# One opening stage for a two-block network's kernel: set-up, first modulation, scales and norm merged, loads in another order, the step-size products moved behind the first weight slot

## The chip, the cores and the metric

The kernel runs on one core of one Trainium2 chip. A core has TensorE (PE in the profile, matmuls; its weight loads are listed apart as PEld), VectorE (DVE), ScalarE (ACT), GpSimd (POOL) and SyncE (SP, which here only issues DMA transfers). The metric is the device time of one execution in microseconds, lower is better: the median of 3 runs is 2491.7 us (2485.37 to 2492.45).

## The reference, cut to what matters

The network is two blocks on x of 256 tokens by 1024 features. The change is at the very start of the first one: the modulation of layer 0, its RMS norm, and the first projection of the hybrid mixer.

```python
cs = jax.nn.silu(c)                                    # c: 1024 values
mod = cs @ ada_w[0] + ada_b[0]                         # 6 x 1024 values
sh1, sc1, g1, sh2, sc2, g2 = split(mod, 6)
h = rms_norm(x, norm_mix_g[0]) * (1 + sc1) + sh1       # rms_norm = x * rsqrt(mean(x*x) + 1e-6) * g
x = x + g1 * hybrid_mixer(h, hy_w_in, ...)             # starts with h @ hy_w_in: z, xBC, dt, q, k, v
...                                                    # ffn, conformer layer, ffn, second block
```

`dt` is the mixer's step size, 32 columns of the projection. `rel_table` gives the attention's bias by distance; the kernel looks it up with one small product against a one-hot matrix.

## The kernel before, in words

All data is fp32, with features on the 128 partitions: x and h are tiles [128, 8, 256]. Weights stream from memory as slots of 128 x 4096 values (2 MB) through a ring of four buffers. `slot_landed[n]` counts their arrival, `slot_used` counts how many were consumed, and SP issues the load of slot n+4 when slot n has been used (`load_ahead`, L97). SP issues everything for the ring, one after the other, on one DMA queue; POOL issues other loads on its own queue.

The program is a row of stages. Each is a `Block` with one instruction list for each engine, and no engine starts a stage before all engines have ended the one before (the branch with which an engine enters a stage waits on a barrier of all five). Within a stage only semaphores order the engines. The stages at the start are:

1. `stage_setup` (L131): SP issues the loads of the vector c (`y<-in_cvec`, copied to all partitions), of ring slots 0 to 3, of the parameters `par`, of the constants `con` and of x, in this order. ACT waits for c, par and con together (`landed`, 48) and applies silu to c.
2. `stage_mod` (L159): DVE computes 16 columns of shift and scale from ring slots 0 to 3, four tiles of 128 x 1024 for each slot (`mod_tile`, L154: multiply and sum in one instruction, written over the weights, followed by a short read of the sum). SP loads the next four slots, the first four of the in-projection, as the ring comes free.
3. `stage_scales` (L255): one DVE instruction, gain = (1 + scale) * g.
4. `stage_norm` (L188, body L193 to L252): ACT squares x in two halves; PE first runs `keep_warm` (two 128x512 products whose result nobody reads), then sums the squares by eight products with a matrix of ones, then seven more `keep_warm` products; DVE scales the sum, ACT takes the root, DVE the reciprocal and x * rstd, and the eight tiles of h are made by DVE and ACT, four each.
5. `stage_hyin` (L280): SP loads `wdt`, the weights of the step sizes, and three small tables. PE computes the step-size products (L339, 16 products 128x32), the look-up (L343), and then ten slots of the in-projection (L271, 32 products of 128x256 for each slot) into two alternating pairs of PSUM banks. DVE copies the step sizes and the masked bias, then for each slot does two modulation tiles of the later columns (weights by POOL's queue), two convolution steps and the copy of one bank; ACT copies the other bank. The third slot's products wait for the first slot's two copies, and so on. After its last ring load SP stores the masked bias (`bias_table`), which the stage waits for at its end.

An fp32 product appears in the trace as two PE records: 32 products of a slot are 64 records.

Of the kernel before, what the change touches and what calls it, by code (L numbers as in the profile page):

```python
# [91 lines left out]
def wait_slot(k, eng, n, turn=0):  # L92

    eng.wait_ge(k.slot_landed[n % RING], turn * 16 + 16 * (n // RING + 1))
# [27 lines left out]
def row(k, name, i=0, n=1):  # L122
    c = PAR[name] + i
    return k.par[:, c:c + n]


def const(k, name):
    return k.con[:, CON[name]:CON[name] + P]


def stage_setup(nc, k, a, cvec):  # L131

    with ExitStack() as ctx:
        landed = ctx.enter_context(nc.semaphore("setup_landed"))
        silu_done = ctx.enter_context(nc.semaphore("setup_silu"))
        block = ctx.enter_context(nc.Block())

        @block.sync
        def _(sp):
            sp.dma_start(cvec, a["cvec"][:, 0:D].to_broadcast([P, D])).then_inc(landed, 16)  # L140
            for n in range(RING):
                sp.dma_start(k.ring[:, n, :], k.stream[n]).then_inc(k.slot_landed[n], 16)
            sp.dma_start(k.par[:], a["par"]).then_inc(landed, 16)
            sp.dma_start(k.con[:], a["con"]).then_inc(landed, 16)
            sp.dma_start(k.x[:], a["xt"]).then_inc(k.x_landed, 16)
            sp.wait_ge(landed, 48)

        @block.scalar
        def _(act):
            act.wait_ge(landed, 48)  # L150
            nc.scalar.activation(cvec, cvec, ACT.Silu).then_inc(silu_done, 1)


def mod_tile(nc, products, w, vec, out, bias):  # L154

    return nc.vector.tensor_tensor_reduce(products, w, vec, 1.0, bias, ALU.mult, ALU.add, out)  # L156


def stage_mod(nc, k, first, vec, out, bias):  # L159


    with ExitStack() as ctx:
        block = ctx.enter_context(nc.Block())

        @block.sync
        def _(sp):
            load_ahead(k, sp, first, RING)
            sp.wait_ge(k.x_landed, 16)

        @block.vector  # L170
        def _(dve):
            for j in range(RING):
                wait_slot(k, dve, first + j)
                w = k.ring[:, (first + j) % RING, :]
                for q in range(4):
                    c = 4 * j + q
                    wt = w[:, q * D:(q + 1) * D]
                    ins = mod_tile(nc, wt, wt, vec, out[:, c:c + 1], bias[:, c:c + 1])
                ins.then_inc(k.slot_used, 1)


def keep_warm(k, pe, bank, n):

    for _ in range(n):
        pe.matmul(k.psum[bank][:], const(k, "ident"), k.con[:, 0:512], start=True, stop=True)  # L185


def stage_norm(nc, k, src, nt, width, scale, bias, dst, name):  # L188
# [91 lines left out]
def stage_hyin(nc, k, h, y, a, dtok, vec, table):  # L280
# [7 lines left out]
    with ExitStack() as ctx:  # L288
# [44 lines left out]
        @block.tensor  # L333
        def _(pe):
            rhs = [h[:, kt, :] for kt in range(KT)]
            pe.wait_ge(wdt_landed, 16)
            for c in range(2):
                for kt in range(KT):
                    mm = pe.matmul(k.psum[7][:, c * HEADS:(c + 1) * HEADS], h[:, kt, c * P:(c + 1) * P],  # L339
                                   wdt[:, kt, :], start=(kt == 0), stop=(kt == KT - 1))  # L340
            mm.then_inc(dt_done, 1)
            pe.wait_ge(bias_in, 48)
            pe.matmul(k.psum[6][0:48, 0:384], rel[:], onehot[:], start=True, stop=True).then_inc(looked_up, 1)  # L343
            for n in range(NFIRST):
                if n >= 2:
                    pe.wait_ge(stored_dve, n - 1)
                    pe.wait_ge(stored_act, n - 1)
                b = 2 * (n % 2)
                outs = [k.psum[b + i // 2][:, (i % 2) * T:(i % 2 + 1) * T] for i in range(4)]
                slot_products(k, pe, first + n, 0, rhs, outs).then_inc(k.slot_used, 1)  # L350

        @block.vector
        def _(dve):
            dve.wait_ge(dt_done, 1)
            nc.vector.tensor_copy(dtok[:], k.psum[7][:, 0:2 * HEADS])
            dve.wait_ge(looked_up, 1)
            nc.vector.scalar_tensor_tensor(flat[:], k.psum[6][0:48, 0:384], 8.0, neg[:], ALU.mult, ALU.add).then_inc(
                bias_masked, 1)

            def half_slot(n):  # L360
                dve.wait_ge(mod_landed, 16 * (n + 1))
# [28 lines left out]
            for n in range(NFIRST):  # L390
                for half in range(*HALVES[n]):
                    half_slot(half)
                for p in turns(n):
                    convolve(p)
                dve.wait_ge(k.slot_used, first + n + 1)
                nc.vector.tensor_copy(y[:, place(n):place(n) + 2, :],
                                      k.psum[2 * (n % 2)].rearrange("p (i t) -> p i t", i=2)).then_inc(stored_dve, 1)

        @block.scalar
        def _(act):  # L400
# [2225 lines left out]
def first_block(nc, k, a):  # L2626
    with ExitStack() as lay:
        h = lay.enter_context(nc.sbuf_tensor("h", [P, KT, T], F32))
        with nc.sbuf_tensor("y", [P, NY, T], F32) as y:
            vec = y[:, ST_V:ST_V + 4, :].rearrange("p i t -> p (i t)")  # L2630
            stage_setup(nc, k, a, vec)
            stage_mod(nc, k, FIRST["mod0"], vec, k.mod[:, 0:16], row(k, "adab0", 0, 16))
            stage_scales(nc, k, [(k.gain[:, 0:8], k.mod[:, 8:16], row(k, "nmix0", 0, 8))])
            stage_norm(nc, k, k.x[:], KT, T, k.gain[:, 0:8], k.mod[:, 0:8], h, "mix0")
# [12 lines left out]
        stage_norm(nc, k, k.x[:], KT, T, row(k, "final1", 0, 8), None, k.x, "final1")  # L2647
# [172 lines left out]
```

## Time and profile before

| | |
|---|---|
| median of 3 runs | 2491.7 us |
| the profiled execution, its own time | 2497.76 us |
| its span in the profile | 2496.1 us |
| PE busy | 2240.5 us (90%) |
| PEld busy | 1643.2 us (66%) |
| DVE busy | 1001.0 us (40%) |
| ACT busy | 530.7 us (21%) |
| mean granted TensorE clock | 0.939 of full speed |
| DMA, mean over the span | 144 GB/s |

The profiled execution has a time of its own, 1.7 us above its span. In the page's row of 40 slices (62 us each) PE is busy for two tenths of the first slice and for six tenths or more of every other one. The stretch that the change touches is the first slice and the one after it.

### The profile page before, as it was taken

What the parts mean: (1) busy time and instruction counts of PE and PEld (TensorE: products, weight loads), DVE (VectorE), ACT (ScalarE), POOL (GpSimd) and SP (SyncE); (2) the same over time, 40 slices, a digit from 0 to 9 for tenths busy, and PEclk for the clock granted to TensorE, in tenths of its full rate; (3) what the DMA queues carried; (4) which work ended last, traced back from release to release, by engine and by line L of the source; (5) the groups of instructions that cost most, each with busy time, mean ns of one, the idle gap of its engine ahead of it and who ended that gap; (6) DMA issues with size and microseconds to landing.
All of it is one profiled execution on the core that took longest, in us unless ns stands there. A gap on an engine that the chain in (4) does not pass through costs nothing. (4 is left out here: it accounts for less than half of the span.)

```text
span 2496.1 us, 39647 instructions
## 1 busy us (share of the span) xinstructions
PE 2240.5 (90%) x16688; PEld 1643.2 (66%) x16688; DVE 1001.0 (40%) x2256; ACT 530.7 (21%) x939; POOL 313.6 (13%) x536
## 2 busy tenths in 40 slices
PE   2998997999999998999986799999998899879898
PEld 1887886787888776888842355556666665446556
DVE  3451633534430572776070533433433531230252
ACT  1112220311000102100022344333333322011151
POOL 0000000000000300000007533342431020000000
PEclk9998998999999999999988899998998799989989
DMA  7454336437854311676026645545443252103000
GB/s 307 175 200 153 113 137 210 93 140 283 304 230 170 132 52 62 277 302 252 34 80 251 194 125 145 144 133 122 136 131 76 56 197 86 68 5 135 34 1 17
DMA packets 127132, 359.76 MB, mean 144 GB/s; under 512 B 78696, under 2 KB 87144, under 8 KB 109424
## 3 DMA queue, kind: packets, MB, share of 16 engines
q1 hardware_dynamic: 93776, 209.90, 24.6%
q0 software_dynamic: 32608, 146.31, 17.3%
q8 instruction: 133, 2.18, 0.4%
q10 hardware_dynamic: 576, 1.05, 0.1%
q14 instruction: 39, 0.32, 0.0%
HBM read 340.36 MB, written 16.85 MB: 143 GB/s over the span
## 5 line engine op out<-in xcount | busy, mean ns | idle before, releaser
L271 PE MATMUL bank<-h,ring 128*128 128x256 f32 x2304 | 500.2, 380 | 4.8 <-DVEq L1074 3.3
L271 PEld LDWEIGHTS bank<-h,ring 128*128 128x128 f32 x2304 | 438.8, 191 | 68.3 <-DVEq L1074 4.9
L1927 PE MATMUL bank<-rw_feed 128*128 128x512 f32 x464 | 258.8, 667 | 27.4 <-DMA rw_feed<-in_rkvg 27.2
L185 PE MATMUL bank<-con 128*128 128x512 f32 x250 | 121.1, 634 | 77.3 <-PEq L257 57.1
L1714 POOL DMA_DIRECT2D rw_feed<-rwkv_mixes x232 | 124.8, 538 | 505.0 <-PE bank L1927 494.6
L2230 DVE TENSOR_TENSOR rw_u<-bank,rw_lam 128x128 f32<-128x128 f32 x120 | 34.9, 291 | 328.4 <-PE bank L1846 325.6
L984 PE MATMUL bank<-ffn_hidden,ring 128*128 128x256 f32 x704 | 152.4, 379 | 3.4 <-PEq L1010 3.4
L488 PE MATMUL bank<-h,ring 128*128 128x256 f32 x640 | 145.9, 386 | 8.3 <-PEq L288 8.3
L984 PEld LDWEIGHTS bank<-ffn_hidden,ring 128*128 128x128 f32 x704 | 133.6, 190 | 22.2 <-issue 4.1
L1927 PEld LDWEIGHTS bank<-rw_feed 128*128 128x128 f32 x464 | 81.3, 203 | 99.0 <-issue 53.3
L488 PEld LDWEIGHTS bank<-h,ring 128*128 128x128 f32 x640 | 122.2, 193 | 28.2 <-issue 11.9
L185 PEld LDWEIGHTS bank<-con 128*128 128x128 f32 x250 | 49.3, 201 | 135.5 <-issue 134.8
L1715 POOL DMA_DIRECT2D rw_feed<-in_rkvg x232 | 124.5, 537 | 9.7 <-issue 9.7
L156 DVE CUSTOM_DVE_ANT_0 next_w<-next_w,next_vec,par 128x1024 f32<-128x1024 f32 x96 | 120.1, 1280 | 11.4 <-DMA next_w<-in_mod_stream 11.4
L996 DVE SCALAR_TENSOR_TENSOR x<-bank,mod,x 128x256 f32<-128x256 f32 x24 | 9.9, 476 | 176.4 <-PE bank L984 176.4
L1846 PEld LDWEIGHTS bank<-rw_u,rw_gr 64*64 64x64 f32 x896 | 36.5, 139 | 65.6 <-issue 63.2
L1198 DVE SCALAR_TENSOR_TENSOR cv_v<-cv_u,par,cv_v 128x256 f32<-128x256 f32 x150 | 67.4, 483 | 22.8 <-DVE cv_v L1198 21.7
L2311 PE MATMUL bank<-mla_h,ring 128*128 128x256 f32 (+1 forms) x240 | 68.3, 449 | 6.5 <-PEq L196 6.5
L1069 ACT ACTIVATE ffn_gate<-bank 128x512 f32<-128x512 f32 x22 | 13.1, 597 | 279.0 <-PE bank L271 279.0
L1854 PE MATMUL bank<-rw_gr,rw_u 64*64 64x32 f32 x960 | 64.2, 223 | 4.4 <-DVE rw_u L2230 4.4
L156 DVE CUSTOM_DVE_ANT_0 next_products<-next_w,next_vec,par 128x1024 f32<-128x1024 f32 x48 | 61.4, 1280 | 12.0 <-DMA next_w<-in_mod_stream 11.9
L2311 PEld LDWEIGHTS bank<-mla_h,ring 128*128 128x128 f32 x240 | 47.3, 198 | 27.9 <-issue 22.6
(414 smaller groups left out, 3409.3 us busy)
## 6 DMA issues: line engine op xcount, KB each, us to landing
ring<-in_stream SPq DMA_DIRECT2D x79, 2048.0 KB, 8.0
rw_feed<-rwkv_mixes POOLq DMA_DIRECT2D x232, 256.0 KB, 3.0
next_w<-in_mod_stream POOLq DMA_DIRECT2D x24, 2048.0 KB, 9.4
ctx<-in_mod_rest POOLq DMA_DIRECT2D x16, 1024.0 KB, 7.0
rw_feed<-in_rkvg POOLq DMA_DIRECT2D x232, 64.0 KB, 3.3
rwkv_mixes<-mixed SPq DMA_DIRECT2D x8, 1024.0 KB, 3.9
y<-bias_table SPq DMA_DIRECT2D x48, 128.0 KB, 5.0
rw_at<-rw_at_kept SPq DMA_DIRECT2D x16, 256.0 KB, 5.3
```

The lines of the kernel that those rows point to most:

```text
L156: return nc.vector.tensor_tensor_reduce(products, w, vec, 1.0, bias, ALU.mult, ALU.add, out)
L185: pe.matmul(k.psum[bank][:], const(k, "ident"), k.con[:, 0:512], start=True, stop=True)
L271: mm = pe.matmul(out, ring_tile(k, n, kt, i * P), rhs[kt], start=start and kt == kts[0], stop=stop and kt == kts[-1])
L488: mm = pe.matmul(k.psum[6 + pair % 2][:, (t % 2) * T:(t % 2 + 1) * T], ring_tile(k, n, kt, (t % 4) * P), h[:, kt, :], start=(kt == 0), sto ...
L984: mm = pe.matmul(k.psum[grp * 4 + i][:, 0:T], ring_tile(k, n, kt, i * P), rhs[part * KT + kt], start=(part == 0 and kt == 0), stop=(part = ...
L1198: nc.vector.scalar_tensor_tensor(v[:, i:i + 1, :], u[:, i:i + 1, bass.ds(t * U + j, T)], k.par[:, bass.ds(t * U + (PAR["dw"] + i * (TAPS + ...
L1714: pool.dma_start(feed[:, g % FEED, 0:512], mixes[j, :, g % KT, :]).then_inc(fed[g % FEED], 16)
L1715: pool.dma_start(feed[:, g % FEED, 512:], a["rkvg"][j, n, :, g % KT, :]).then_inc(fed[g % FEED], 16)
L1846: mm = pe.matmul(k.psum[c % 2][rows64(e), 64 * d:64 * d + 64], GR[n % 2][d][rows64(e), c, 0:64], U[rows64(e), c % 2, d, :], start=False, s ...
L1854: mm = pe.matmul(k.psum[2 + c % 2][rows64(e), at:at + 32], U[rows64(e), c % 2, d, :], GR[n % 2][d][rows64(e), c, 64:96], start=(d == 0), s ...
L1927: pe.matmul(k.psum[PROJ], feed[:, g % FEED, 512:], feed[:, g % FEED, 0:512], start=(kt == 0), stop=(kt == KT - 1)).then_inc(eaten, 1)
L2311: mm = pe.matmul(out, ring_tile(k, n, kt, i * P), rhs[kt], start=(kt == 0), stop=(kt == KT - 1))
```

## The change

`stage_setup`, `stage_mod`, `stage_scales` and `stage_norm` of this place become one stage, `stage_opening`. Its SP list issues c, par, slot 0, x, con, slots 1 to 3 and then the next four slots as the ring comes free. ACT's silu waits for c and par alone. DVE's instructions of the norm stand between its modulation tiles. PE has no products ahead of the sum of squares; behind it stand 14 `keep_warm` products that wait until three slots have been used. In `stage_hyin` the step-size products and the look-up, and DVE's two instructions on their results, stand behind the first slot. What is computed is the same.

```diff
-def stage_setup(nc, k, a, cvec):
...
-            for n in range(RING):
-                sp.dma_start(k.ring[:, n, :], k.stream[n]).then_inc(k.slot_landed[n], 16)
-            sp.dma_start(k.par[:], a["par"]).then_inc(landed, 16)
-            sp.dma_start(k.con[:], a["con"]).then_inc(landed, 16)
-            sp.dma_start(k.x[:], a["xt"]).then_inc(k.x_landed, 16)
-            sp.wait_ge(landed, 48)
...
-def stage_mod(nc, k, first, vec, out, bias):
...
+def stage_opening(nc, k, a, vec, h):
+    first = FIRST["mod0"]
...
+        shift, scale = k.mod[:, 0:8], k.gain[:, 0:8]
+        block = ctx.enter_context(nc.Block())
+
+        @block.sync
+        def _(sp):
+            sp.dma_start(vec, a["cvec"][:, 0:D].to_broadcast([P, D])).then_inc(landed, 16)
+            sp.dma_start(k.par[:], a["par"]).then_inc(landed, 16)
+            sp.dma_start(k.ring[:, 0, :], k.stream[0]).then_inc(k.slot_landed[0], 16)
+            sp.dma_start(k.x[:], a["xt"]).then_inc(k.x_landed, 16)
+            sp.dma_start(k.con[:], a["con"]).then_inc(con_landed, 16)
+            for n in range(1, RING):
+                sp.dma_start(k.ring[:, n, :], k.stream[n]).then_inc(k.slot_landed[n], 16)
+            load_ahead(k, sp, first, RING)
 
         @block.scalar
         def _(act):
+            act.wait_ge(landed, 32)
+            nc.scalar.activation(vec, vec, ACT.Silu).then_inc(silu_done, 1)
+            act.wait_ge(k.x_landed, 16)
+            for lo in (0, KT // 2):
+                nc.scalar.activation(sq[:, lo:lo + KT // 2, :], k.x[:, lo:lo + KT // 2, :], ACT.Square).then_inc(squared, 1)
+            act.wait_ge(step, 1)
+            nc.scalar.activation(rstd[:], rstd[:], ACT.Sqrt).then_inc(rooted, 1)
+            act.wait_ge(gained, 1)
+            for i in range(1, KT, 2):
+                nc.scalar.activation(h[:, i, :], sq[:, i, :], ACT.Identity, bias=shift[:, i:i + 1], scale=scale[:, i:i + 1])
+
+        @block.tensor
+        def _(pe):
+            pe.wait_ge(con_landed, 16)
+            for i in range(KT):
+                if i % (KT // 2) == 0:
+                    pe.wait_ge(squared, 2 * i // KT + 1)
+                mm = pe.matmul(k.psum[0][:, 0:T], const(k, "ones"), sq[:, i, :], start=(i == 0), stop=(i == KT - 1))
+            mm.then_inc(summed, 1)
+            pe.wait_ge(k.slot_used, first + RING - 1)
+            keep_warm(k, pe, 7, 14)
 
         @block.vector
         def _(dve):
...
+            dve.wait_ge(silu_done, 1)
+            mods(0)
+            dve.wait_ge(summed, 1)
+            s(nc.vector.tensor_scalar(rstd[:], k.psum[0][:, 0:T], 1.0 / D, EPS, ALU.mult, ALU.add))
+            mods(1)
+            dve.wait_ge(rooted, 1)
+            s(nc.vector.reciprocal(rstd[:], rstd[:]))
+            s(nc.vector.tensor_tensor(sq[:], k.x[:], rstd[:].unsqueeze(1).to_broadcast([P, KT, T]), ALU.mult))
+            mods(2)
+            mods(3)
+            dve.wait_ge(k.slot_used, first + RING)
+            nc.vector.scalar_tensor_tensor(scale, k.mod[:, 8:16], 1.0, row(k, "nmix0", 0, 8), ALU.add, ALU.mult).then_inc(
+                gained, 1)
+            dve.wait_ge(gained, 1)
+            for i in range(0, KT, 2):
+                nc.vector.tensor_scalar(h[:, i, :], sq[:, i, :], scale[:, i:i + 1], shift[:, i:i + 1], ALU.mult, ALU.add)
...
                 slot_products(k, pe, first + n, 0, rhs, outs).then_inc(k.slot_used, 1)
+                if n == 0:
+                    pe.wait_ge(wdt_landed, 16)
...
+                    mm.then_inc(dt_done, 1)
+                    pe.wait_ge(bias_in, 48)
+                    pe.matmul(k.psum[6][0:48, 0:384], rel[:], onehot[:], start=True, stop=True).then_inc(looked_up, 1)
```

`mods(j)` is the body of the old `stage_mod` for one slot: it waits for the slot, runs four `mod_tile` and adds one to `slot_used`. `s(...)` issues one instruction of DVE and waits for its end.

In the three pairs below each row is one instruction, or several alike (x8); L is the line, then the operation, what it writes and what it reads. SP, start of the program, before:

```order
L140 DMA y<-in_cvec 128x1024
L142 DMA ring<-in_stream 128x4096 x4
L143 DMA par<-in_par 128x790
L144 DMA con<-in_con 128x768
L145 DMA x<-in_xt 128x2048
```

And now:

```order
L159 DMA y<-in_cvec 128x1024
L160 DMA par<-in_par 128x790
L161 DMA ring<-in_stream 128x4096
L162 DMA x<-in_xt 128x2048
L163 DMA con<-in_con 128x768
L165 DMA ring<-in_stream 128x4096 x3
L102 DMA ring<-in_stream 128x4096 x4
```

par moves ahead of all ring slots, x and con ahead of slots 1 to 3; the bytes are the same. PE from the program's start to the second slot of the in-projection, before (its 320 products are the ten slots):

```order
L185 MATMUL bank<-con 128x512 x2
L230 MATMUL bank<-norm_sq_mix,con 128x256 x8
L185 MATMUL bank<-con 128x512 x7
L196 UNCONDITIONAL_BRANCH
L333 UNCONDITIONAL_BRANCH
L339 MATMUL bank<-hyin_wdt,h 128x32 x16
L343 MATMUL bank<-bias_onehot,bias_rel 48x384
L271 MATMUL bank<-h,ring 128x256 x320
```

And now:

```order
L187 MATMUL bank<-open_sq,con 128x256 x8
L139 MATMUL bank<-con 128x512 x14
L146 UNCONDITIONAL_BRANCH
L368 UNCONDITIONAL_BRANCH
L306 MATMUL bank<-h,ring 128x256 x32
L382 MATMUL bank<-hyin_wdt,h 128x32 x16
L386 MATMUL bank<-bias_onehot,bias_rel 48x384
L306 MATMUL bank<-h,ring 128x256 x288
```

Two products ahead of the sum are gone, seven behind it have become fourteen, and the step sizes stand between the first slot's 32 products and the other 288. DVE behind the last modulation tile of slot 3, before:

```order
L162 UNCONDITIONAL_BRANCH
L260 UNCONDITIONAL_BRANCH
L263 SCALAR_TENSOR_TENSOR gain<-mod,par 128x8
L257 UNCONDITIONAL_BRANCH
L235 UNCONDITIONAL_BRANCH
L240 TENSOR_SCALAR norm_rstd_mix<-bank 128x256
L244 RECIPROCAL norm_rstd_mix<-norm_rstd_mix 128x256
L245 TENSOR_TENSOR norm_sq_mix<-x,norm_rstd_mix 128x2048
L249 TENSOR_SCALAR h<-norm_sq_mix,gain,mod 128x256 x4
```

And now, from the same tile on:

```order
L216 SCALAR_TENSOR_TENSOR gain<-mod,par 128x8
L220 TENSOR_SCALAR h<-open_sq,gain,mod 128x256 x4
L146 UNCONDITIONAL_BRANCH
L388 UNCONDITIONAL_BRANCH
```

The scaling of the sum now stands behind slot 0's tiles and the reciprocal and the product behind slot 1's; behind slot 3's only the gain and the tiles of h are left.

## Rows read from the trace of the kernel before

**Rows 1.** The page, busy time of each engine.

```profile
PE 2240.5 (90%) x16688; PEld 1643.2 (66%) x16688; DVE 1001.0 (40%) x2256; ACT 530.7 (21%) x939; POOL 313.6 (13%) x536
```

**Rows 2.** Waits, 0 to 120 us: engine, line <- awaited: us, times, longest.

```profile
PE bank L185 <- PEq L257: 49.2, 1, 49.2
ACT y L151 <- DMA con<-in_con: 24.9, 1, 24.9
```

**Rows 3.** DMA issues, first 6 us: how many, KB, median us to landing.

```profile
y<-in_cvec SPq DMA_DIRECT2D x1, 512.0 KB, 4.6
x<-in_xt SPq DMA_DIRECT2D x1, 1024.0 KB, 24.7
```

**Rows 4.** Windows: us, busy of PE, PEld, DVE, ACT, POOL; PEclk, DMA, GB/s.

```profile
10.00:15.00 5.00, 0.00 (x0) 0.00 (x0) 0.00 (x0) 0.00 (x0) 0.00 (x0) 1.00 1.01 429
```

**Rows 5.** Timeline to 64 us: start, us, engine, line, tiles, count [idle before].

```profile
0.89 0.39 SPq L140 DMA_DIRECT2D y<-in_cvec  x1
...
4.82 0.44 SPq L145 DMA_DIRECT2D x<-in_xt  x1
...
28.48 1.28 DVE L156 CUSTOM_DVE_ANT_0 ring<-ring,y,par 128x1024 f32<-128x1024 f32 x1 [28.48 <-PEq L133]
...
33.31 1.28 DVE L156 CUSTOM_DVE_ANT_0 ring<-ring,y,par 128x1024 f32<-128x1024 f32 x1
...
48.71 0.17 DVE L263 SCALAR_TENSOR_TENSOR gain<-mod,par 128x8 f32<-128x8 f32 x1 [0.84 <-PEq L162]
...
49.16 2.00 ACT L210 ACTIVATE norm_sq_mix<-x 128x1024 f32<-128x1024 f32 x2 [21.03 <-PEq L257]
49.18 3.75 PE L185 MATMUL bank<-con 128*128 128x512 f32 x4 [49.18 <-PEq L257]
...
52.73 4.32 PE L230 MATMUL bank<-norm_sq_mix,con 128*128 128x256 f32 x16
...
56.89 6.17 PE L185 MATMUL bank<-con 128*128 128x512 f32 x14
57.09 0.42 DVE L240 TENSOR_SCALAR norm_rstd_mix<-bank 128x256 f32<-128x256 f32 x1 [8.21 <-PE bank L230]
...
58.07 1.75 DVE L244 RECIPROCAL norm_rstd_mix<-norm_rstd_mix 128x256 f32<-128x256 f32 x1 [0.56 <-ACT norm_rstd_mix L213]
...
59.86 2.29 DVE L245 TENSOR_TENSOR norm_sq_mix<-x,norm_rstd_mix 128x2048 f32<-128x2048 f32 x1
...
62.19 2.07 ACT L218 ACTIVATE h<-norm_sq_mix,mod,gain 128x256 f32<-128x256 f32 x4 [4.22 <-DVE norm_sq_mix L245]
```

**Rows 6.** Timeline, 64 to 104 us.

```profile
64.51 0.33 SPq L316 DMA_DIRECT2D hyin_wdt<-in_wdt  x1
...
66.63 6.00 PE L339 MATMUL bank<-hyin_wdt,h 128*128 128x32 f32 x32 [3.57 <-DMA hyin_wdt<-in_wdt]
...
72.56 1.51 PE L343 MATMUL bank<-bias_onehot,bias_rel 32*48 32x384 f32 x2
...
74.01 36.35 PE L271 MATMUL bank<-h,ring 128*128 128x256 f32 x158
...
90.10 0.69 DVE L396 COPY y<-bank 128x512 f32<-128x512 f32 x1 [13.03 <-PE bank L271]
...
103.92 0.69 DVE L396 COPY y<-bank 128x512 f32<-128x512 f32 x1 [3.66 <-PE bank L271]
```

**Rows 7.** Windows, PE alone: us, busy (records), granted clock, DMA, GB/s.

```profile
67.00:68.00 1.00, 1.00 (x11) 0.90 0.73 282
68.00:69.00 1.00, 1.00 (x6) 0.50 1.01 422
...
78.00:79.00 1.00, 1.00 (x6) 0.98 0.47 66
```

**Rows 8.** Windows, PE alone, at a later pause of PE.

```profile
241.50:242.00 0.50, 0.00 (x0) 0.88 0.51 197
```

**Rows 9.** Timeline, first product behind the in-projection's first ten slots.

```profile
222.66 16.80 PE L488 MATMUL bank<-h,ring 128*128 128x256 f32 x64 [8.28 <-PEq L288]
```

More of the change, by code:

```diff
@@ L128, in const, with mod_tile, keep_warm, sem @@
     return k.con[:, CON[name]:CON[name] + P]
-def stage_setup(nc, k, a, cvec):
-    with ExitStack() as ctx:
-        landed = ctx.enter_context(nc.semaphore("setup_landed"))
-        silu_done = ctx.enter_context(nc.semaphore("setup_silu"))
+def mod_tile(nc, products, w, vec, out, bias):
+    return nc.vector.tensor_tensor_reduce(products, w, vec, 1.0, bias, ALU.mult, ALU.add, out)
+def keep_warm(k, pe, bank, n):
+    for _ in range(n):
+        pe.matmul(k.psum[bank][:], const(k, "ident"), k.con[:, 0:512], start=True, stop=True)
+def stage_opening(nc, k, a, vec, h):
+    first = FIRST["mod0"]
+    with ExitStack() as ctx:
+        sq = ctx.enter_context(nc.sbuf_tensor("open_sq", [P, KT, T], F32))
+        rstd = ctx.enter_context(nc.sbuf_tensor("open_rstd", [P, T], F32))
+        def sem(name):
+            return ctx.enter_context(nc.semaphore("open_" + name))
+        landed, con_landed, silu_done, squared, summed, rooted, step, gained = (sem(n) for n in (
+            "landed", "con_landed", "silu_done", "squared", "summed", "rooted", "step", "gained"))
+        shift, scale = k.mod[:, 0:8], k.gain[:, 0:8]
         block = ctx.enter_context(nc.Block())
@@ L154, in mod_tile @@
-def mod_tile(nc, products, w, vec, out, bias):
-    return nc.vector.tensor_tensor_reduce(products, w, vec, 1.0, bias, ALU.mult, ALU.add, out)
-def stage_mod(nc, k, first, vec, out, bias):
[L162 to L168, printed above, removed]
+            act.wait_ge(landed, 32)
+            nc.scalar.activation(vec, vec, ACT.Silu).then_inc(silu_done, 1)
@@ L170, in _, with mods @@
+        @block.tensor
[8 more added lines that the diff above has]
+            keep_warm(k, pe, 7, 14)
         @block.vector
         def _(dve):
-            for j in range(RING):
+            s = Steps(dve, step)
+            def mods(j):
@@ L177, in _ @@
                     wt = w[:, q * D:(q + 1) * D]
-                    ins = mod_tile(nc, wt, wt, vec, out[:, c:c + 1], bias[:, c:c + 1])
+                    ins = mod_tile(nc, wt, wt, vec, k.mod[:, c:c + 1], row(k, "adab0", c))
                 ins.then_inc(k.slot_used, 1)
-def keep_warm(k, pe, bank, n):
-    for _ in range(n):
-        pe.matmul(k.psum[bank][:], const(k, "ident"), k.con[:, 0:512], start=True, stop=True)
+            dve.wait_ge(silu_done, 1)
[14 more added lines that the diff above has]
+                nc.vector.tensor_scalar(h[:, i, :], sq[:, i, :], scale[:, i:i + 1], shift[:, i:i + 1], ALU.mult, ALU.add)
 def stage_norm(nc, k, src, nt, width, scale, bias, dst, name):
@@ L335, in _ @@
             rhs = [h[:, kt, :] for kt in range(KT)]
[L336 to L343, printed above, removed]
             for n in range(NFIRST):
@@ L350, in _ @@
                 slot_products(k, pe, first + n, 0, rhs, outs).then_inc(k.slot_used, 1)
+                if n == 0:
+                    pe.wait_ge(wdt_landed, 16)
+                    for c in range(2):
+                        for kt in range(KT):
+                            mm = pe.matmul(k.psum[7][:, c * HEADS:(c + 1) * HEADS], h[:, kt, c * P:(c + 1) * P],
+                                           wdt[:, kt, :], start=(kt == 0), stop=(kt == KT - 1))
+                    mm.then_inc(dt_done, 1)
+                    pe.wait_ge(bias_in, 48)
+                    pe.matmul(k.psum[6][0:48, 0:384], rel[:], onehot[:], start=True, stop=True).then_inc(looked_up, 1)
         @block.vector
         def _(dve):
[L354 to L358, printed above, removed]
             def half_slot(n):
@@ L397, in _ @@
                                       k.psum[2 * (n % 2)].rearrange("p (i t) -> p i t", i=2)).then_inc(stored_dve, 1)
+                if n == 0:
+                    dve.wait_ge(dt_done, 1)
+                    nc.vector.tensor_copy(dtok[:], k.psum[7][:, 0:2 * HEADS])
+                    dve.wait_ge(looked_up, 1)
+                    nc.vector.scalar_tensor_tensor(flat[:], k.psum[6][0:48, 0:384], 8.0, neg[:], ALU.mult,
+                                                   ALU.add).then_inc(bias_masked, 1)
         @block.scalar
@@ L2630, in first_block @@
             vec = y[:, ST_V:ST_V + 4, :].rearrange("p i t -> p (i t)")
[L2631 to L2634, printed above, removed]
+            stage_opening(nc, k, a, vec, h)
             stage_hybrid(nc, k, a, h, y, vec)
```

3 lines of the change are left out of this document (removed).

## The prediction, made before the changed kernel ran

> **What bounds the kernel now.** The page's engine line comes first: PE is busy 90% of the span and no other engine half of it [rows 1]. So a change pays if PE begins its dense work earlier or runs it at the full clock, and what is won at the start should reach the end undiminished: the reader is to look for a time at which PE has finished a given product, before and after. I take the end of the in-projection's second slot, since the second slot is the first piece of PE's work ahead of which the two versions have done the same.
>
> The waits of the first 120 us say why PE is late: it stands idle for 49.2 us, until DVE's gain instruction lets the norm stage begin, and ACT waits 24.9 us for con, which lies behind 8 MB of ring slots although the silu doesn't read it [rows 2]. The timeline then gives the old path. DVE starts its 16 modulation tiles at 28.48; four take 33.31 - 28.48 = 4.83 us. Gain at 48.71, squares at 49.16, and PE puts two idle products (3.75 us) ahead of the sum. Scaling, root, reciprocal and x * rstd follow, and the last tile of h ends at 62.19 + 2.07 = 64.26 [rows 5]. The next stage begins at once (SP issues at 64.51), but PE waits 3.57 us in all for wdt; slot 0 is done at 90.10 and slot 1 at 103.92, as DVE's copies show, 13.82 us later [rows 6].
>
> The clock matters in two places. In the windows it reads 1.00 until 67 us, falls during the step-size products, to 0.50 (1.2 GHz), and is back at 78 [rows 7]. But the granted clock is not all: the first two idle products at 49.18 took 1.87 us each, the seven later ones 0.88 each. The eight 128x256 products of the sum took 4.32 us, where 0.44 each (half of 0.88) would give 3.5 and 0.94 each 7.5: some 1.6 of them were still slow, so PE ran at half speed until about 49.18 + 3.55 + 1.6 * 0.94 = 54.2, for 5.0 us from its first product [rows 5].
>
> **Loads.** At 429 GB/s [rows 4] a ring slot of 2048 KB (2.10 MB) takes 4.9 us, x 2.4, par (790 columns, 395 KB) and con 0.9 each. c lands at 0.89 + 4.6 = 5.5 [rows 3, 5]. Check on the old order: everything behind c is 9995 KB, 23.9 us, so x at 29.4; it landed at 4.82 + 24.7 = 29.5 [rows 3, 5]. In the new order: par 6.4, slot 0 11.3, x 13.7, con 14.6, slot 1 19.5, slot 2 24.4, slot 3 29.3. The four in-projection slots queue behind (asked for at 16.2, 26.6, 35.6, 40.5) and the last is in by 49; SP has nothing else in this stage.
>
> The Trainium skill, DMA: Bandwidth & Descriptors, section "Queues, rings and completion order", says that each DMA engine takes the descriptors of a ring in order, though completions needn't be in order. By it x lands ahead of slots 1 to 3, as in my sum; the 29.5 above agrees.
>
> **DVE and the sum of squares.** Silu of a 128x1024 tile should be like a square of that size, 1.0 us [rows 5], done by 7.5, under the load of slot 0. DVE's slot 0: 11.4 to 16.2. ACT squares from 13.8 to 15.8, PE starts the sum at 15.0, at half speed: 5.0 us hold 5.3 products, the other 2.7 take 1.2, end 21.2 (all fast 18.5, all slow 22.5; the trace shows no sum begun cold, and I take the nearest row, the 5.0 us). DVE waits for it, behind which all its tiles are queued; since slot 1 lands at 19.5 only 1.7 us of the 5.0 are lost. Scaling 0.42, slot 1 to 26.6, reciprocal and product 62.19 - 58.07 = 4.12 [rows 5] to 30.8, slot 2 to 35.6, slot 3 to 40.5. Root and its table load lie beside slot 1. Gain 0.3 with its hand-over, h 2.07: h is ready at 42.9, 21.4 us sooner than before.
>
> **The fourteen idle products.** They begin when slot 2 is used, 35.7, with PE idle since 21.2 and so cold. Seven cost 6.17 us warm and two 3.75 cold [rows 5]. With 5.0 us at half speed, 2.8 products, and 11.2 at 0.87: 14.7 us, to 50.4. All warm they would cost 12.3 (to 48.0), all cold 26.2 (to 61.9). Even the lower bound is 5 us behind h. PE takes its instructions in order, so this run and not h sets the start of the projection; 7.5 of h's 21.4 us are given back. Hand-over from one stage to the next: 49.18 - 48.88 = 0.3 [rows 5]. Slot 0 starts at 50.7.
>
> **The in-projection.** Slot 0 now runs warm, 13.8 us, to 64.5; wdt and the tables arrive under it, so the 3.57 us wait is gone. Step sizes: 32 records at the 11 in a microsecond seen ahead of the fall [rows 7] make 2.9 us, against 6.00; look-up 0.76, half of 1.51 [rows 6]; to 68.2. Slot 1: 13.8, to 82.0, against 103.92. Saved: 21.9 us, 13.9 up to the start of the stage and 8.0 in it (wait and hand-over 2.1, step sizes 3.1, look-up 0.7, slot 0 2.3 where it ran at half clock until 78).
>
> The unknown is the clock behind the step sizes. Nowhere before do such narrow products follow dense ones. If they count as a pause, the clock may fall as at 67.9, or at 242 within 2 us of PE going idle [rows 8]. Then the rest of them and a part of slot 1 run at half: 1.5 us at the least, and at the most all of step sizes and look-up slow (3.8 more) and slot 1 slow for 4 us (2 more), 5.8. Above zero a gain is excluded, since they are reckoned warm.
>
> DVE in slot 1: its modulation half and convolutions now stand behind the step sizes' copies, which start 3.7 us after slot 0's end and take under 1. Before, it waited 3.66 us for slot 1 [rows 6]; PE's slot 1 ends later by those same 3.7 us. So some 3 us of cover are left. If it were gone PE still wouldn't stop there, since slot 2 waits for slot 0's copies only; slot 3 is the first that waits for slot 1's. The masked bias is stored behind SP's last ring load, in a pause of 8.28 us at the stage's end [rows 9], as before.
>
> **Sum.** 2497.76 of the profiled execution less 21.9 is 2475.9. The median of the runs shown is 6.1 lower than that execution: 2491.7 - 21.9 = 2469.8.
>
> **Rivals.**
> - The clock falls at the step sizes: 21.9 less 1.5 to 5.8, so 2471.3 to 2475.6, say 2473.5. For it: at half clock these products didn't bring it back from 68 to 74 [rows 6, 7]. Against: dense work lies right ahead and behind.
> - The loads don't land in order, x only with the last ring slot. Squares at 31, sum 37, then slots 1 to 3 and 4.1: slot 2 used at 51.7, idle products to 66.4, slot 1's end at 98.0. Saved 5.9: 2485.8. Against: the 29.5 of the check.
> - Later phases of the clock shift. The program has many pauses of a few microseconds, after which PE is sometimes slow and sometimes not; all later ones move by 22 us. By rows 6 and 7 one fall costs some 2 to 5 us, so a net of one more or less is 3: 2467 or 2473. It widens the others more than it is a case.
> - Slower: the clock falls at the step sizes and stays down over the slots behind. Each costs 13.8 more. From 1.6 slots on nothing is left, from 2.2 it is slower than 0.3%; three slots: 2491.7 - 21.9 + 41.4 = 2511.2. Against: with dense products from 74.0 the clock was back by 78 [rows 6, 7].
>
> The Trainium skill, TensorE: Matmul & The Clock Gate, section "The HAM clock gate", reports the gate stuck at a quarter of the clock for over 50 us. At a quarter, 50 us do 12.5 us of work: 37.5 lost, 2507. No row here shows a quarter; I give it less than 0.01, within the slower case.
>
> **Chances.** Forecast 0.62, the fall at the step sizes 0.27, loads late 0.05, slower 0.02; 0.04 for gains beyond it (warmer idle products 2.4, and a fall fewer later, to 2464). A measurement can tell about 0.3%, 7.5 us: faster means below 2484.2. Both first cases and the last are faster; of the late loads a third. Faster 0.93, same 0.05, slower 0.02. Range: 2462 to 2479: the cases' 2464 to 2475.6 and some 3 us for how far single runs lie apart.
>
> **What would show it.** In the changed profile: x lands near 14; DVE's first tile at 11.4, its gain near 40.6; 28 records of 128x512 from 35.7 to about 50.4, two or three products of them slow, with h done 7 us earlier; PE's first projection product at 50.7; step sizes in 3 us at clock 1.00; slot 1's copy at 82. The forecast is wrong if slot 0 starts before 48 or after 53, if the clock shows 0.50 between 64 and 82, or if the shift of 22 us at slot 1 isn't found again at the end.

## The result and the profile after

The changed kernel takes 2454.7 us (median of 4 runs, 2451.3 to 2459.5) against 2492.1 us for the kernel before beside it (2485.4 to 2493.5): a ratio of 0.9855, 95% interval 0.9832 to 0.9879. It is faster, as forecast, but by 37.4 us and not by 21.9: 2454.7 lies 15 us under the forecast of 2469.8 and below its range. The profiled execution took 2451.3 us, its span is 2449.6 us and the mean granted clock 0.948, against 2497.8, 2496.1 and 0.939.

The page after, busy time of each engine, which answers to [rows 1]:

```profile
PE 2219.7 (91%) x16698; PEld 1631.1 (67%) x16698; DVE 1000.5 (41%) x2256; ACT 529.9 (22%) x939; POOL 312.7 (13%) x536
```

PE is busy 20.8 us less, with ten records more in the trace: part of the gain is faster products, not less waiting. The waits from 0 to 120 us, against [rows 2] (engine, line, what it waited for: us, times, longest):

```profile
PE bank L187 <- ACT open_sq L174: 15.0, 1, 15.0
PEld bank L187 <- DMA con<-in_con: 15.0, 1, 15.0
PE bank L139 <- DVE mod L133: 14.4, 1, 14.4
```

PE's one wait of 49.2 us has become two, 29.4 in all. The DMA issues of the first 6 us, against [rows 3] (how many, KB, median us to landing):

```profile
x<-in_xt SPq DMA_DIRECT2D x1, 1024.0 KB, 11.5
y<-in_cvec SPq DMA_DIRECT2D x1, 512.0 KB, 4.3
```

x lands at 2.27 + 11.5 = 13.8, the 13.7 of the sum. The timeline after, against [rows 5, 6] (start, us, engine, line, tiles, count, idle before):

```profile
11.42 1.28 DVE L133 CUSTOM_DVE_ANT_0 ring<-ring,y,par 128x1024 f32<-128x1024 f32 x1 [11.42 <-DMA ring<-in_stream]
...
13.79 2.00 ACT L174 ACTIVATE open_sq<-x 128x1024 f32<-128x1024 f32 x2 [6.36 <-DMA x<-in_xt]
...
14.99 5.15 PE L187 MATMUL bank<-open_sq,con 128*128 128x256 f32 x16 [14.99 <-ACT open_sq L174]
...
20.18 0.42 DVE L208 TENSOR_SCALAR open_rstd<-bank 128x256 f32<-128x256 f32 x1 [3.85 <-PE bank L187]
...
34.55 14.20 PE L139 MATMUL bank<-con 128*128 128x512 f32 x28 [14.40 <-DVE mod L133]
...
39.35 0.17 DVE L216 SCALAR_TENSOR_TENSOR gain<-mod,par 128x8 f32<-128x8 f32 x1
39.55 2.08 ACT L179 ACTIVATE h<-open_sq,mod,gain 128x256 f32<-128x256 f32 x4 [18.50 <-DVE gain L216]
...
49.04 14.05 PE L306 MATMUL bank<-h,ring 128*128 128x256 f32 x64 [0.30 <-PEq L146]
...
62.93 3.65 PE L382 MATMUL bank<-hyin_wdt,h 128*128 128x32 f32 x32
63.13 0.69 DVE L427 COPY y<-bank 128x512 f32<-128x512 f32 x1 [5.59 <-PE bank L306]
66.52 0.84 PE L386 MATMUL bank<-bias_onehot,bias_rel 32*48 32x384 f32 x2
...
81.40 0.69 DVE L427 COPY y<-bank 128x512 f32<-128x512 f32 x1 [4.00 <-PE bank L306]
```

Slot 1's copy stands at 81.40, against 103.92: 22.5 us saved where the sum said 21.9. The windows of PE alone, against [rows 7] (us, busy and records, granted clock, DMA, GB/s), keep the full clock:

```profile
65.00:67.00 2.00, 2.00 (x17) 1.00 0.87 344
67.00:68.00 1.00, 1.00 (x5) 1.00 0.84 360
```

**Where the spans part behind slot 1.** Same instructions of DVE, looked up in both traces, cut the 46.5 us between the two spans into five. The rwkv scan is the long recurrence in the second block, whose stage runs there with PE busy in short pieces (the marks at 1861 and 2039 us of before are two executions of the line that ends as `TENSOR_TENSOR rw_u<-bank,rw_lam`, in the rwkv scan):

| piece (us of before) | before | before, a second trace | after | saved, first trace |
|---|---|---|---|---|
| to slot 1's copy | 103.9 | 103.7 | 81.4 | 22.5 |
| to 1406.6, in the rwkv scan | 1302.7 | 1302.9 | 1299.7 | 3.0 |
| to 1861.3 | 454.7 | 447.5 | 444.0 | 10.7 |
| to 2039.2 | 177.9 | 177.8 | 168.0 | 9.9 |
| to the end | 456.9 | 457.0 | 456.5 | 0.4 |

From slot 1 until 1378 us the shift stays between 22.3 and 23.3 us: ffn and conformer layer run as before, earlier. All the rest of what was not forecast arises in the rwkv scan. The third piece differs by 7.2 us between two traces of one program; the fourth by 0.1. So the fourth is a difference between programs, and it is what most experiments below go after.

### The profile page after: what moved, and what is told of

It reads as the page before. It is cut to its first block and busy times, and to the rows that moved or that the text cites. A ratio compares the mean times of both kernels' runs of the same rounds, so it can differ in the third digit from the quotient of the medians.

```text
span 2449.6 us, 39635 instructions
## 1 busy us (share of the span) xinstructions
PE 2219.7 (91%) x16698; PEld 1631.1 (67%) x16698; DVE 1000.5 (41%) x2256; ACT 529.9 (22%) x939; POOL 312.7 (13%) x536
## 5 line engine op out<-in xcount | busy, mean ns | idle before, releaser
L1964 PE MATMUL bank<-rw_feed 128*128 128x512 f32 x464 | 251.4, 651 | 22.9 <-DMA rw_feed<-in_rkvg 22.5
L133 DVE CUSTOM_DVE_ANT_0 next_w<-next_w,next_vec,par 128x1024 f32<-128x1024 f32 x96 | 120.0, 1279 | 11.4 <-DMA next_w<-in_mod_stream 11.4
```

The lines of the kernel that those rows point to most:

```text
L1964: pe.matmul(k.psum[PROJ], feed[:, g % FEED, 512:], feed[:, g % FEED, 0:512], start=(kt == 0), stop=(kt == KT - 1)).then_inc(eaten, 1)
```

## The experiments

All ratios are against the kernel before, run beside each on the same chip. "Rest" is the span behind slot 1's copy.

**1 and 2. Both kernels again, to have two traces of each.**

> The kernel before, unchanged, for a second profile and more times. Both theories expect the second slot of the in-projection done at 103.9 us. Theory A (the 15 us that the change gained beyond its own stretch come from where the TensorE clock's falls happen to lie in the rwkv scan, which differs from execution to execution): the scan's course in this profile differs from the first profile's, and the time from the second slot's end to the end of the program lies anywhere between 2368 and 2394 us. Theory B (the program after the change runs its later stages differently, each time): that time is 2381 to 2394 us, as in the executions of before so far.

Measured: 2490.7 us, ratio 0.9994 (0.9974 to 1.0014); slot 1 at 103.7, rest 2385.2.

> The kernel after, unchanged, for a second profile and more times. Second slot done at 81.4 us. Theory A (chance of the clock's phase): the rest takes anything between 2368 and 2394 us, median of the runs drifting up towards 2470. Theory B (later stages differ systematically): the rest takes 2368 to 2378 us again, total 2450 to 2460.

Measured: 2458.9 us, ratio 0.9864 (0.9841 to 0.9886); rest 2371.9; but slot 1 at 85.31, not 81.40. Windows of PE alone and timeline of this repeat:

```profile
66.00:67.00 1.00, 1.00 (x9) 0.75 0.99 393
67.00:68.00 1.00, 1.00 (x5) 0.50 0.88 377
68.00:73.00 5.00, 5.00 (x11) 0.50 0.51 218
```

```profile
63.57 4.19 PE L382 MATMUL bank<-hyin_wdt,h 128*128 128x32 f32 x32
67.68 1.51 PE L386 MATMUL bank<-bias_onehot,bias_rel 32*48 32x384 f32 x2
...
63.77 0.69 DVE L427 COPY y<-bank 128x512 f32<-128x512 f32 x1 [5.44 <-PE bank L306]
...
85.31 0.69 DVE L427 COPY y<-bank 128x512 f32<-128x512 f32 x1 [6.06 <-PE bank L306]
```

The clock falls to 0.50 for 6.8 us under the end of the step sizes and the start of slot 1. From copy to copy that is 85.31 - 63.77 = 21.5 us, against 81.40 - 63.13 = 18.3: 3.3 us. So the same program does either, and the first profile had shown the lucky one. Of the ten traces in this study with the step sizes behind slot 0, seven show a fall there (in six of 6.8 us, in one of 3.4), three none.

**3. The changed kernel, begun later.** A DVE chain ahead of the opening, ten instructions, some 24 us:

```diff
+            stage_delay(nc, k, h[:], y[:, 0:KT, :], 9)   # memset, then 9 products 128x2048
             stage_opening(nc, k, a, vec, h)
```

> The kernel after, with an empty piece ahead of everything: DVE fills a tile and squares it nine times (about 22 us), and only then the opening stage begins. So every later instruction is the changed kernel's, but at the old kernel's time. Second slot done at about 104 us. If the later stages depend on when they run since the program's start, the rest takes 2381 to 2394 us and the total is 2485 to 2498. If they depend on the program's own instructions, the rest takes 2368 to 2378 us and the total is 2473 to 2482.

Measured: 2484.2 us, ratio 0.9957 (0.9937 to 0.9976); slot 1 at 109.33 (with a fall at the step sizes), later than in the kernel before, and yet the whole is some 10 us faster than it (2494.4 us in this comparison): rest 2372.2, in the range expected if the program's own instructions decide. The total is 2 us above its expected range, as slot 1 came 5 us later than expected. The gain behind slot 1 doesn't come from being early.

**4. The step sizes alone** behind slot 0, in the kernel before.

```diff
-            pe.wait_ge(wdt_landed, 16)
-            ...                                  # step sizes, look-up
             for n in range(...):
                 slot_products(k, pe, first + n, 0, rhs, outs).then_inc(k.slot_used, 1)
+                if n == 0:
+                    pe.wait_ge(wdt_landed, 16)
+                    ...                          # step sizes, look-up
```

> The kernel before with one part of the change alone: step-size products and look-up behind the first slot. Theory of the terms: the 2.1 us wait goes, the step sizes take 3 instead of 6 us, the look-up 0.8 instead of 1.5, slot 0 runs at full clock (2.3 us less): second slot done at 95.9 instead of 103.9; at 99 to 100 if the clock falls at the step sizes. The rest of the program: if its 12 to 15 us less in the kernel after come from this part, 2368 to 2377 us, otherwise 2377 to 2395 as in the kernel before.

Measured: slot 1 at 96.31, 7.6 us saved, as the sum's terms have it (8.0). Step sizes 3.65 us, no fall, rest 2381.3, as expected if the gain behind slot 1 doesn't come from this part. Time 2486.2 us, ratio 0.9992 (0.9966 to 1.0017): 7.6 us would be 0.9970, inside the interval, so the whole time can't tell it from nothing.

**5. The step sizes undone** in the changed kernel, the opening kept (the diff of 4, reversed).

> The kernel after with the same part undone: step sizes ahead of the first slot, behind a wait for wdt. Second slot done at 82.7 if the clock holds through the wait (2.1 us for wdt, the rest as in the kernel after less the hand-over), at 86 to 89.5 if it falls there as it did in the kernel before (step sizes 6.0, look-up 1.5, slot 0 16.1). The rest: 2377 to 2395 if its gain comes from the moved step sizes, 2368 to 2377 otherwise.

Measured: 2461.4 us, ratio 0.9889 (0.9854 to 0.9924); slot 1 at 88.75: PE waits 2.25 us for wdt, the step sizes take 6.02 and the look-up 1.51, since the clock falls from 52.6 to 62.9. Rest 2375.3.

**6. The old order of the loads** in the changed kernel.

```diff
-sp: c, par, slot 0, x, con, slots 1 to 3
+sp: c, slots 0 to 3, par, con, x
```

> The kernel after with the loads in the old order (c, ring slots 0 to 3, par, con, x). Theory (the loads' order is what lets DVE begin at 11 us): par lands at 26.0, DVE begins at 27.3, the sum of squares ends at about 36, slot 2 used at 50.1, idle products to 64.8, second slot done at 96.5: 15 us later than in the kernel after. Rival (the merged stage by itself hides most of it): less than 8 us later. The rest 2368 to 2377 unless the loads' order is what shortens it.

Measured: 2474.0 us, ratio 0.9939 (0.9916 to 0.9961). DVE starts at 27.2 instead of 11.4, slot 0 at 65.9 instead of 49.0, slot 1 is done at 101.5 with a fall at the step sizes, 16.2 us behind the repeat, which has one too. The order of the loads is worth 16 of the 22.5 us. What is left here, the moved step sizes and the merged stage with its fourteen idle products, would have slot 1 done at 98.2 without the fall's 3.3 us; the step sizes alone had it at 96.3 (experiment 4). So under the old order of the loads merging wins nothing, as far as one trace of each can say. Rest 2375.6.

**7. Three empty stages** ahead of the opening, since it has three fewer than the four stages it replaces.

```diff
+            for i in range(3):
+                with nc.Block() as block:
+                    @block.vector
+                    def _(dve): pass
             stage_opening(nc, k, a, vec, h)
```

> The kernel after with three empty stages ahead of the opening: each adds a barrier and two to three instructions on every engine, so that the later instructions of DVE and POOL lie within one place of where they lie in the kernel before (they are 8 and 9 fewer in the kernel after). Second slot done at 82 to 83. If the rest of the program is shorter in the kernel after because its instructions lie elsewhere in memory (fetching them collides less), the rest is 2380 to 2395 here. If it has another cause, 2368 to 2377.

Measured: 2465.0 us, ratio 0.9911 (0.988 to 0.9943); slot 1 at 86.64, 1.3 us behind the repeat; rest 2374.8, still short. The stages as such aren't it. By the recorded expectation this also rules out the place of the instructions as the cause. That would be too soon: by the count found below, the wait that matters is number 2355 here and 2353 in the kernel before, so the test missed the place by two.

**8. One tiny instruction more, in the kernel before.** By then the traces had shown one odd place. DVE's timeline of the kernel before:

```profile
1893.64 0.20 DVE L2259 RECIPROCAL rw_rst<-rw_rst 128x8 f32<-128x8 f32 x1 [3.16 <-ACT rw_rst L2134]
1894.30 0.69 DVE L2158 TENSOR_TENSOR ring<-rkv,ring 128x512 f32<-128x512 f32 x1 [0.45 <-issue]
```

"[0.45 <-issue]" says that DVE waited for nothing that the profile shows. Between the two stand three waits on semaphores. The time is lost ahead of the second, whose semaphores had last been raised 20 and 35 us earlier (those of the other two 2 us earlier or more); in the changed kernel the gap is 0.10 us. The edit moves every later DVE instruction by one place:

```diff
         def _(dve):
+            for i in range(1):
+                nc.vector.memset(k.gain[:, 8 + i:9 + i], 0.0)
             for j in range(RING):
```

> The kernel before with one instruction more on DVE: a write of one column of a table that is overwritten later, at the head of the first modulation, while DVE waits for the loads anyway. Nothing else moves; only each later DVE instruction stands one place further on in DVE's program. Theory (the rwkv scan's time is set by DVE's place in its program: at one wait in it, 1894 us into the trace of before, DVE pauses 0.45 instead of 0.10 us although both of its semaphores had long been updated, and TensorE's clock then falls at other places): with 1270 instead of 1269 DVE instructions ahead of the scan, as in the kernel with the three empty stages, the pause is gone and the span behind the copy of slot 1 is about 9 us shorter than the kernel before's 2385 us, so 2376 us, and the time near 2482 us. Rival (the merged opening itself shortens it, by what it leaves in memory, on the queues or in the barriers): nothing changes, 2385 us and 2491 us. Either way slot 1 is done at 103.7 us.

Measured: 2481.9 us, ratio 0.9961 (0.9944 to 0.9979). Slot 1 at 103.67, the gap is 0.10 us, the stretch 168.0 us, rest 2368.5 in the profiled execution, where the theory said 2376. An instruction of 128 values, whose result nobody reads, makes the kernel some 10 us faster (2493.1 us beside it).

**9. Eight in the changed kernel**, at the head of the opening's DVE list, so that as many instructions stand in DVE's program ahead of the scan as in the kernel before.

> The changed kernel with eight such instructions at the head of DVE's opening, ahead of its first modulation tile: DVE has then 1269 instructions ahead of the scan, as many as the kernel before. They cost under 1 us of start, since DVE issues them once c has landed (slot 1 done at 81.4 to 82.2 us, or 3.9 us later where the clock falls at the step sizes). Theory: the pause at the wait in the rwkv scan is back, the two falls of the clock behind it too, and the span behind the copy of slot 1 is about 9 us longer than the changed kernel's 2368 to 2376 us, so 2377 to 2385 us, and the time near 2465 us. Rival (the merged opening itself): 2368 to 2376 us and a time of 2451 to 2459 us.

Measured: 2460.3 us, ratio 0.9865 (0.9839 to 0.9892): no pause, the stretch 168.0 us. The theory as written falls: the place in the written program doesn't decide. Counting what DVE executed (loops unrolled; semaphores, moves and branches too) does better: the kernel before is four instructions ahead of the changed one there, not eight.

**10. Four**, the test of that count.

> The changed kernel with four of the tiny DVE instructions at the head of its opening instead of eight. In the traces so far each place in the rwkv scan at which DVE pauses some 0.35 us longer than in the others has the number 1585, 2225, 2353 or 2481 among the instructions that DVE executed (semaphores, moves and branches counted, loops unrolled), steps of 128: 2225 in the changed kernel and its variants without a pad, 2353 in the kernel before, 2481 in the kernel before with one instruction more. The wait in question is number 2353 in the kernel before, 2354 with one more, 2349 in the changed kernel and 2357 with eight more. Theory: with four more it is number 2353, so the pause comes back there (0.45 instead of 0.10 us), TensorE's clock falls at the two places where it does in the kernel before, and the stretch behind takes about 9 us longer relative to its own start than with eight more; the span behind the copy of slot 1 is 2377 to 2385 us, the time 2459 to 2467 us. Rival 1 (the pause is there but the clock's falls depend on something else): the pause, and 2368 to 2376 us. Rival 2 (the count has nothing to do with it): no pause at that wait, 2368 to 2376 us, a time of 2451 to 2460 us.

Measured: 2471.4 us, ratio 0.9914 (0.9892 to 0.9936). The pause is back; rest 2385.9 and time lie 1 and 4 us above the theory's ranges, far from both rivals. DVE's timeline around the wait, with four:

```profile
1869.57 0.20 DVE L2298 RECIPROCAL rw_rst<-rw_rst 128x8 f32<-128x8 f32 x1 [3.15 <-ACT rw_rst L2173]
1870.23 0.69 DVE L2197 TENSOR_TENSOR ring<-rkv,ring 128x512 f32<-128x512 f32 x1 [0.45 <-issue]
```

and with eight:

```profile
1869.42 0.20 DVE L2298 RECIPROCAL rw_rst<-rw_rst 128x8 f32<-128x8 f32 x1 [3.15 <-ACT rw_rst L2173]
1869.73 0.69 DVE L2197 TENSOR_TENSOR ring<-rkv,ring 128x512 f32<-128x512 f32 x1
```

Ahead of it the two traces lie 0.15 us apart. PE's windows and PE's and DVE's timeline behind it, with four:

```profile
1872.00:1880.00 8.00, 6.33 (x158) 1.00 0.21 52
1880.00:1884.00 4.00, 4.00 (x18) 0.57 1.07 188
1896.00:1910.00 14.00, 14.00 (x158) 0.63 0.09 25
```

```profile
1879.93 1.96 PE L1966 MATMUL bank<-rw_feed 128*128 128x512 f32 x2
...
2015.05 0.29 DVE L2269 TENSOR_TENSOR rw_u<-bank,rw_lam 128x128 f32<-128x128 f32 x1 [3.36 <-PE bank L1885]
```

and with eight:

```profile
1872.00:1880.00 8.00, 6.69 (x154) 1.00 0.24 55
1880.00:1884.00 4.00, 3.04 (x50) 1.00 1.11 200
1896.00:1910.00 14.00, 14.00 (x267) 1.00 0.16 50
```

```profile
1879.43 1.12 PE L1966 MATMUL bank<-rw_feed 128*128 128x512 f32 x2
...
2005.14 0.29 DVE L2269 TENSOR_TENSOR rw_u<-bank,rw_lam 128x128 f32<-128x128 f32 x1 [3.07 <-PE bank L1885]
```

Behind the pause PE has the same rows, each 0.50 us later (0.15 from ahead of the wait and 0.35 of pause: the 128x512 products start at 1879.93 and 1879.43). The window to 1880 holds 0.36 us less of busy PE; that is work that comes later, not work that is gone. Then comes the clock at about half twice (3.4 and 10.2 us), where it stays full with eight, and a third fall of 34.1 instead of 20.5 us; at the next mark the two are 9.9 us apart. All fourteen traces agree:

| traces | number of that wait | gap around it | stretch |
|---|---|---|---|
| before, its repeat, step sizes alone, after with four more | 2353 | 0.45 us | 177.8 to 177.9 us |
| before with one more | 2354 | 0.10 us | 168.0 us |
| after, its repeat, step sizes undone, old loads, 7 idle products | 2349 | 0.10 us | 168.0 to 168.1 us |
| 5 idle products | 2349 | 0.10 us | 165.6 us |
| after with three empty stages; with eight more; begun later | 2355; 2357; 2362 | 0.10 us | 168.0 us |

The trace with 5 idle products has 165.6 us since the last fall of the stretch, 6.8 us in the others, isn't in it. Shown: the number of tiny instructions decides over the pause and over the 9.9 us. That the pause moves the clock's falls, by having PE's work come 0.35 us later, is read from the order of the rows; no experiment made such a gap by another means.

**11 and 12. Fewer idle products** behind the sum of squares, 7 and 5 instead of 14, since these and not h set the start of slot 0.

```diff
-            keep_warm(k, pe, 7, 14)
+            keep_warm(k, pe, 7, 7)     # 11; and 5 in 12
```

> The kernel after with 7 instead of 14 idle products behind the sum of squares. My theory of the opening (the idle products, not h, set the start of the projection): they end 7 x 0.86 = 6.0 us sooner, at 42.7, about when h is ready (41.6); slot 0 starts at 43.1 instead of 49.0, second slot done at 75.4 instead of 81.4. Rival (without the long run the clock is down when slot 0 starts): the second slot is done 2 to 4 us later than that, 77.5 to 79.5. The whole time follows by the same amount, 2446 to 2454, unless the later stages change their course.

Measured: 2449.7 us, ratio 0.9822 (0.9799 to 0.9844). Slot 0 starts at 45.58 instead of 49.04 and runs at the full clock (14.05 us); slot 1 at 77.95. The theory had 43.1 and 75.4. Slot 2 was used at 36.3 instead of 34.6, and the seven products took 8.99 us and not 6.0, as the first of them ran at half clock. So 77.95 falls into the rival's range without its cause: the clock wasn't down when slot 0 started.

> The changed kernel with 5 idle products behind the sum of squares instead of 14. With 7 of them slot 0 started at 45.6 us, with h ready at 43.4 us; five end near 42.7 us if they run at the low clock too (0.64 us a record), so h is what slot 0 waits for, and it starts at 43.4 us. Theory 1 (the clock rises by the work that PE has done since its start, whichever products these are): slot 0 begins at the low clock either way and loses what it won: slot 1 done at 77 to 78.5 us, the same as with 7. Theory 2 (the gap of 0.7 us costs nothing and the rise comes at the same time as before): slot 1 done at 76 us, 2 us earlier than with 7 and 5.5 us earlier than the changed kernel. The time 2446 to 2452 us.

Measured: 2449.0 us, ratio 0.9826 (0.9799 to 0.9852), the fastest with 7. PE's and DVE's timeline with 5:

```profile
35.76 7.09 PE L139 MATMUL bank<-con 128*128 128x512 f32 x10 [14.40 <-DVE mod L133]
...
43.15 14.05 PE L306 MATMUL bank<-h,ring 128*128 128x256 f32 x64 [0.30 <-PEq L146]
...
57.23 0.69 DVE L427 COPY y<-bank 128x512 f32<-128x512 f32 x1 [2.78 <-PE bank L306]
...
77.16 0.69 DVE L427 COPY y<-bank 128x512 f32<-128x512 f32 x1 [5.65 <-PE bank L306]
```

Slot 0 starts at 43.15 and takes the same 14.05 us, so it doesn't begin cold even behind five: theory 1 falls. The granted clock of this trace is 0.51 from 40.0 to 40.9 us and 1.00 from 40.9 on, 2 us before the five end. They end at 42.85 and h at 42.84, so fewer still would win nothing. Theory 2's 76 us missed by 1.2, since a fall of 3.4 us at the step sizes took 77.16 - 57.23 - 18.3 = 1.6.

## Why the prediction was right and wrong

**The sum to slot 1: right.** DVE's start was put at 11.4 and is 11.42; the sum's end at 21.2, it is 14.99 + 5.15 = 20.1; the idle products 35.7 to 50.4, they ran from 34.55 to 48.75; slot 0 at 50.7, it is 49.04; step sizes 2.9, measured 3.65 with no fall; look-up 0.76, measured 0.84; slot 1 at 82.0, it is 81.4. Two errors cancel in part: the opening was 1.7 better, the step sizes and slot 1 some 1 worse. Three small slips stand in the sum's working and move nothing: 5.0 us hold 2.7 slow products of 1.87 and not 2.8; the four parts given for the stage add up to 8.2 and not 8.0; and the chances of the faster cases add up to 0.95 and not 0.93. Experiments 4 to 6 confirm the shares: 7.6 us for the step sizes in the old surroundings (reckoned as 8.0), 16 us for the loads' order (15 expected of that experiment).

**The fall at the step sizes: the mechanism right, its chance too low.** It was given 0.27, and seven of ten traces show it. Its price, 1.5 to 5.8 us, holds: 3.3 us for the fall of 6.8 us, 1.6 for that of 3.4. "If the clock shows 0.50 between 64 and 82" was named as what would make the forecast wrong; it does in the repeat, and costs the forecast 3 us, in the direction away from the measured time.

**The step that failed** is "what is won at the start should reach the end undiminished", and with it the rival "Later phases of the clock shift", which was sized at 3 us and said to widen the others "more than it is a case". Its cause was given as the move of all later pauses by 22 us. Both were wrong. The move in time does nothing that the traces show: the shift keeps within 1 us for 1270 us, and the kernel begun 24 us later keeps the short rest. What counts is which instruction of DVE is the one that pauses. With the pause the old and the new opening have the ratios 0.9994 and 0.9914, without it 0.9961 and 0.9865. So the opening is worth 0.0080 and 0.0096, which is 20 and 24 us of 2492, as forecast, and the pause 0.0033 and 0.0049, 8 and 12 us, whichever opening stands ahead (each ratio is good to about 0.0025, 6 us, so it is the 9.9 us of the traces that sizes the pause). The test named at the end of the prediction, the 22 us found again at the end, is what showed it: 46.5 were found.

Put together for the medians: 22.5 us up to slot 1 and 9.9 us for the stretch make 32.4 of the 37.4. The other 5.0 are open, and with the fall at the step sizes, which the repeat has and which puts slot 1 only 18.6 us ahead, it is up to 9. The profiled spans have 3.0 and 10.7 us in the two pieces ahead of the stretch, but there two traces of the kernel before differ by 7.2 us, and over all fourteen traces the third piece runs from 444.0 to 454.7 us with kernels of both openings at either end; part of it is how executions scatter, and nothing here separates the rest.

**The slower rival and the late loads** didn't come: x landed ahead of slots 1 to 3, and no fall at the step sizes outlasted 6.8 us.

## What to carry to other kernels

Reckon a change locally and trust the sum up to a mark, but then follow the shift of the same instructions to the end: if it grows in a piece that the change doesn't touch, look there, in two traces of each kernel, before crediting the change. A piece that repeats within 0.1 us for one program and differs by 10 us for another has a cause that is worth looking for; add one, four or eight harmless instructions and see whether it moves. And when comparing two versions of a kernel that lives at the edge of the clock, know that adding an instruction far ahead can by itself be worth what it was here, 0.3 to 0.5%.

## What the runs showed of the hardware

**DVE pauses some 0.35 us at fixed steps of its instruction count.** In the scan, the places at which DVE has in some traces 0.2 to 0.4 us more between two instructions than in the others, with nothing to wait for, are numbers 1585 (seven traces), 2225 (after and the five others with its count), 2353 (four) and 2481 (one) of what DVE executed: steps of 128. Far ahead of the scan, with loops between, it shows at 191 and 447 in one trace each and at 971 in nine. At the numbers of this step where nothing is seen, the pause may be covered by a wait or by the instruction before; that isn't shown. The page of the changed kernel lists two queues of a kind of their own (packets, MB, share of 16 engines):

```profile
q8 instruction: 133, 2.18, 0.4%
q14 instruction: 39, 0.32, 0.0%
```

that is 16.4 KB for each packet of the first and 8.2 KB for each of the second. The Trainium skill, Runtime: NRT & Kernel Launch, section "Instruction fetch mechanics", says that an engine's instruction store is refilled in blocks of 16 KiB, 256 instructions, and that crossing a boundary is mostly hidden. The packets of q8 agree. Those of q14 are half of that: 128 instructions each by the page's figure (an estimate), which is the step at which DVE pauses. The counts fit q8 to PE and q14 to the other engines: 133 times 256 is 34,048 beside the 33,396 of PE and PEld on the page, and 39 times 128 is 4,992. In the four traces with the pause at 2353 a packet of q14 starts 0.7 us behind it, but the first one behind the pause at 2225 comes 3.5 to 4.1 us later, and the trace doesn't say whose packet it is. That the refill is the cause of the pause isn't shown, only the step. The pause that isn't hidden costs 0.35 us at the spot, and where the clock's course changes with it 10 us; the one at 2225 has no such change in the six traces that have it.

**With a gap of a third of a microsecond the clock takes another course for the next 90 us.** With and without it the granted clock differs in three places (3.4, 10.2 and 13.6 us more at half), and each pattern repeats in every trace of its group.

**Behind five 128x512 products (7.09 us) the dense slot runs as fast as behind fourteen** (14.20 us): slot 0 takes 14.05 us after either.
